# A two-part network on one core: an opening that starts its products early, meta tiles padded to 128 rows, and the last pair's norm taken head by head

## The reference, cut to what matters

```python
def first_block(...):                      # DEPTH = 2
    h = concatenate([meta, x], axis=1)     # 16 + 512 tokens
    for i in range(DEPTH):
        hn = rmsnorm(h, norm_w[i])
        h = h + (pool_mixer(hn, ...) if i == 0 else hgrn2_mixer(hn, ...))
    return rmsnorm(h[:, N_META:], final_norm_w)

def rmsnorm(x, w):
    return x * rsqrt(mean(x * x, -1) + EPS) * w

def pool_mixer(h, w_in, w_grp, scale, w_out):
    v, gate = split(h @ w_in, 2)           # 2 x 2048 columns, in 4 groups
    ...                                    # trailing means of v over 2, 4, 8 or 16 tokens, minus v
    return (u * silu(gate)) @ w_out

def hgrn2_mixer(h, w_in, lb, o_norm, w_out):
    q, fp, i_in, gate = split(h @ w_in, 4)  # 16 heads of 128
    # per head: gated linear attention in chunks, o = (scores @ v) + q * decay @ S
    o = o * rsqrt(mean(o * o, -1) + EPS)    # over each head's 128 values
    return (o * o_norm * silu(gate)) @ w_out
```

## Time and profile before

| | |
|---|---|
| median of 3 runs | 1637.94 us (1637.83 to 1638.79) |
| the profiled execution, its own time | 1639.15 us |
| its span, first to last instruction | 1637.3 us |
| TensorE busy | 1604.7 us (98%) |
| weight loads, VectorE, ScalarE, POOL busy | 85%, 60%, 34%, 24% |
| mean granted TensorE clock | 0.997 |

### The profile page before, as it was taken

One profiled execution on the slowest core, in us unless ns is written; L12 is line 12 of the kernel. 1 busy time (PEld: TensorE's weight loads), 2 busy tenths in 40 slices (PEclk: granted clock), 3 DMA queues, 4 the chain that ended last, 5 costly groups with the idle time before them and its releaser, 6 DMA issues.

```text
span 1637.3 us, 31100 instructions
## 1 busy us (share of the span) xinstructions
PE 1604.7 (98%) x12926; PEld 1398.9 (85%) x12926; DVE 989.8 (60%) x1524; ACT 548.9 (34%) x965; POOL 389.0 (24%) x344
## 2 busy tenths in 40 slices
PE   6999999999999999999999899999999999999998
PEld 5999999998888888889888688777888887778886
DVE  6757575765766568475675454557624845575446
ACT  4322222243243232324334333554112226451121
POOL 0000000020422124031431314327350043254510
PEclk9999999999999999999999999999999999999999
DMA  4323232323211312221222133222233242123331
GB/s 135 104 78 104 78 103 78 104 78 109 71 61 53 106 53 79 78 79 54 77 79 91 53 102 92 78 76 78 90 117 129 76 137 78 52 78 103 103 118 63
DMA packets 112619, 142.17 MB, mean 87 GB/s; under 512 B 3068, under 2 KB 88480, under 8 KB 112480
## 3 DMA queue, kind: packets, MB, share of 16 engines
q1 hardware_dynamic: 108368, 133.07, 25.4%
q10 hardware_dynamic: 4032, 6.89, 1.3%
q0 software_dynamic: 80, 0.20, 0.0%
HBM read 137.01 MB, written 2.10 MB: 85 GB/s over the span
## 4 chain that ended last, share of the span: by engine, by line
PE 93%; DVE 3%; ACT 2%; issue 1%; DMA 0%; SPq 0%; POOL 0%; DVEq 0%; ACTq 0%; POOLq 0%
PE acc L371 27%; PE acc L373 25%; PE acc L372 25%; PE aux L525 2%; PE aux L1098 1%; PE aux L1122 1%; PE aux L1109 1%; PE aux L371 1%; PE aux L372 1%; PE aux L373 1%; PE aux L552 1%; PE aux L550 1%; PE aux L511 1%; PE aux L542 1%; PE aux L430 0%
## 5 line engine op out<-in xcount | busy, mean ns | idle before, releaser
L371 PE MATMUL acc<-xhis,whi 128*128 128x264 f32 (+2 forms) x1888 | 627.9, 333 | 3.7 <-issue 1.1
L372 PE MATMUL acc<-xlos,whi 128*128 128x264 f32 (+2 forms) x1888 | 613.5, 325 | 0.0
L373 PE MATMUL acc<-xhis,wlo 128*128 128x264 f32 (+2 forms) x1888 | 613.5, 325 | 0.0
L371 PEld LDWEIGHTS acc<-xhis,whi 128*128 128x128 f32 x1888 | 355.4, 188 | 39.7 <-issue 7.1
L373 PEld LDWEIGHTS acc<-xhis,wlo 128*128 128x128 f32 x1888 | 355.5, 188 | 30.1
L372 PEld LDWEIGHTS acc<-xlos,whi 128*128 128x128 f32 x1888 | 355.8, 188 | 26.3
L366 POOL TENSOR_TENSOR wlo<-raw,whi 128x1024 fp32r<-128x1024 f32 x84 | 207.6, 2473 | 373.4 <-DVE whi L1931 373.4
L362 ACT ACTIVATE whi<-raw 128x1024 fp32r<-128x1024 f32 x160 | 165.9, 1048 | 152.8 <-PE acc L373 138.0
L366 DVE TENSOR_TENSOR wlo<-raw,whi 128x1024 fp32r<-128x1024 f32 x83 | 101.9, 1234 | 35.4 <-ACT whi L362 35.4
L1931 DVE CAST whi<-raw 128x1024 fp32r<-128x1024 f32 x84 | 66.3, 793 | 69.6 <-PE acc L373 66.6
L1728 DVE TENSOR_TENSOR wlo<-raw,whi 128x1024 fp32r<-128x1024 f32 x77 | 95.3, 1241 | 19.0 <-ACT whi L362 18.8
(11 more groups left out here) (281 smaller groups left out, 2644.0 us busy)
## 6 DMA issues: line engine op xcount, KB each, us to landing
raw<-in_w_in SPq DMA_DIRECT2D x38, 1024.0 KB, 5.1
raw<-in_hgrn_w_in SPq DMA_DIRECT2D x32, 1024.0 KB, 5.7
raw<-in_pool_w_in SPq DMA_DIRECT2D x16, 1024.0 KB, 5.4
raw<-in_pool_w_out SPq DMA_DIRECT2D x8, 1024.0 KB, 5.0
raw<-in_hgrn_w_out SPq DMA_DIRECT2D x8, 1024.0 KB, 5.1
raw<-in_w_out SPq DMA_DIRECT2D x8, 1024.0 KB, 5.0
raw<-in_pool_w_grp SPq DMA_DIRECT2D x4, 1024.0 KB, 5.2
raw<-in_w_branch_attn SPq DMA_DIRECT2D x4, 1024.0 KB, 4.9
```

Source lines behind the costliest of these rows:

```text
L371: pe.matmul(dst, stat[0], mov[0], start=first, stop=False)
L372: pe.matmul(dst, stat[0], mov[1], start=False, stop=False)
L373: return pe.matmul(dst, stat[1], mov[0], start=False, stop=last)
```

## The change

**Meta tiles of 128 rows.** `vtm` and `ktm` have 128 partitions in place of 16. POOL clears them once; ScalarE goes on writing their first 16 rows, and the matmul of L540 takes all 128.

**Last pair.** The norm is made head by head: squares, mean, reciprocal and root of head 0, its scaling by VectorE, then head 1 with scaling by ScalarE. A root of a dummy value is put behind the states' step. The second two pieces of weights are split by VectorE after level 7 instead of after level 6. In all pairs POOL's last level multiplies k of both heads before it combines their gates.

**b_out and the mean.** The last split and last gate product of the even pair (`held`) move behind the first addition to `h`. `mean_squares` runs within the second half of the first unit of stage B and not after it.

**Opening.** The identity and the norm weights are loaded first, then the first chunk of weights; the second waits for the last part of x. x comes in four parts of 256 features. TensorE begins with 14 matmuls on the matrix of ones. The sums of squares are taken by ScalarE along the rows of x (`row_squares`), 5 numbers per partition; the root and reciprocal are made of those, and a diagonal matrix times the matrix of ones (`spread_inverse`) gives `rstd`. The first two v units are made together, k-tile by k-tile as x comes in (`v_pair`). The gates' lower bounds are computed in stage A's first "out" part.

```diff
-            vtm = [sb(f"vtm{x}", [META, P], where=in_b) for x in range(2)]
+            vtm = [sb(f"vtm{x}", [P, P], where=in_b) for x in range(2)]
...
-            ktm = [sb(f"ktm{x}", [META, P], where=in_b) for x in range(2)]
+            ktm = [sb(f"ktm{x}", [P, P], where=in_b) for x in range(2)]
...
+                    if late is not None and n == 1 and k == K // 2 - 1:
+                        late()
...
-                    if first:
-                        mean_squares()
...
+            load_chunk(sp, 0, 0, w_in_a[:, :, 0:256], "k8", 0)
...
+                        if g == 0 and n == 1:
+                            sp.wait_ge(x_landed[3], 16)
...
+            for n in range(WARM):
+                pe.matmul(aux[:, n % 2, 0:P], ones_d[:, :], ones_d[:, :], start=True, stop=True)
...
+            def v_pair():
+
+                for k in range(6):
+                    turn(k)
+                pe.wait_ge(vec_ready, 1)
+                pe.wait_ge(meta_ready, 1)
+                pe.wait_ge(lo_ready, PA + 1 + CREDIT)
+                v_products(0, (0, 1))
+                turn(6)
+                v_products(0, (2, 3))
+                turn(7)
+                pe.wait_ge(lo_ready, PA + 2 + CREDIT)
+                v_products(1, (0, 1, 2, 3))
+                for tiles in ((4, 5), (6,)):
+                    for n in range(2):
+                        v_products(n, tiles)
+                spread_inverse()
+                for n in range(2):
+                    v_products(n, (7,)).then_inc(lin_done, 1)
+                vectors()
...
+            row_squares(0)
...
+            x_high(0)
+            x_high(1)
+            x_high(2)
+            split_hi(act, "k8", 0, 16, None)
+            x_high(3)
+            row_squares(1)
...
+                if s == LEVELS + 3:
+                    act.activation(spare[:, 1:2], ones_d[:, 0:1], ACT.Sqrt)
...
+                    if n == 0:
+                        held()
...
-                b_pair(i, "even", (2 * i + 1, 1), "k4")
-                b_out(UB + 24 + B_STEPS * i, PB + 24 + B_PIECES * i, True)
+                held = b_pair(i, "even", (2 * i + 1, 1), "k4", True)
+                b_out(UB + 24 + B_STEPS * i, PB + 24 + B_PIECES * i, True, held)
...
-                if s in (6, 7):
+                if s in (6, 8):
                     for m in range(2):
-                        split_lo_at(PO3, m + 2 * (s - 6), "vg")
+                        split_lo_at(PO3, m + s - 6, "vg")
```

More of the change, by code:

```diff
@@ L410, in weighted_lo, with root, inverse_vector, x_turned @@
                                      in1=xhi[:, k, :], op0=ALU.mult, op1=ALU.subtract).then_inc(xlo_ready, 1)
[L412 to L431, removed]
[L432 to L438 removed]
+        def root(act):
+            act.wait_ge(ms_ready, 2)
+            act.activation(rstd[:, :], rstd[:, :], ACT.Sqrt).then_inc(rstd_ready, 1)
+        def inverse_vector(dve):
+            dve.wait_ge(sq_used, 1)
+            dve.tensor_scalar(halves(rstd[:, :]), aux[:, :, 0:TH], EPS, None, ALU.add).then_inc(ms_ready, 1)
+            dve.wait_ge(ms_ready, 1)
+            dve.reciprocal(rstd[:, :], rstd[:, :]).then_inc(ms_ready, 1)
+            dve.wait_ge(rstd_ready, 1)
+        def x_turned(k):
+            return (aux, aux2)[k % 4 // 2][:, k % 2, :]
         def x_wait(pe, v):
@@ L555, in b_tensor_step @@
                 else:
-                    pe.wait_ge(on_ready, 1 + 2 * pair + x + 1)
+                    if z == "last" and x:
+                        pe.wait_ge(on_second, 1)
+                    else:
+                        pe.wait_ge(on_ready, 1 + 2 * pair + x + 1)
                     for c in range(CH):
@@ L878, in _ @@
                     pair = 2 * i + par
-                    for level in range(1, LEVELS + 1):
+                    for level in range(1, LEVELS):
                         for x in range(2):
@@ new lines, in spread_inverse, with v_products @@
+            def spread_inverse():
+                pe.wait_ge(h_ready, KT)
+                pe.wait_ge(diag_ready, 2)
+                pe.matmul(aux[:, 0, :], ones_d[:, :], diag[:, :, :].rearrange("p c t -> p (c t)"),
+                          start=True, stop=True)
+                pe.matmul(aux[:, 1, 0:META], ones_d[0:META, :], diag_m[:, :], start=True, stop=True)\
+                  .then_inc(spread, 1)
+            def v_products(n, tiles):
+                hi, lo = piece(whi, "k8", n), piece(wlo, "k8", n)
+                for k in tiles:
+                    pe.wait_ge(xlo_ready, k + 1)
+                    for half in range(2):
+                        mm = products(pe, acc[n][:, half, 0:TH], (hi[:, k, 0:P], lo[:, k, 0:P]),
+                                      of_x(k, TH * half, TH), k == 0, k == KT - 1)
+                return mm
@@ L1297, in _ @@
                         a_split(i, m)
+                    if stage == "out" and G == 0 and n == 4:
+                        act.wait_ge(lb_step, 3)
+                        act.activation(lbt[:, 3:5, :], lbt[:, 1:3, :], ACT.Exp).then_inc(lb_exp, 1)
                     if stage == "out" and G == NG - 1:
```

275 lines of the change are left out of this document (190 added, 85 removed).

## The result

| | before | after |
|---|---|---|
| median (times in the same set of runs) | 1638.15 us (1637.83 to 1638.79) | 1615.05 us (1614.13 to 1616.31) |
| ratio | | 0.9859, 95% interval 0.9842 to 0.9876 |
| the profiled execution, and its span | 1639.15, 1637.3 | 1616.31, 1614.5 |

The change makes the kernel 23.1 us faster by the medians and 22.8 by the spans. 1613.7 was predicted, with a range from 1609.5 to 1619.0.

What follows compares the result with a forecast made beforehand. TensorE, busy for 98% of the span, was taken as the bound. Terms of 6.2, 2.2, 1.0, 3.6, 3.4 and 7.8 sum to 24.2 us: 1639.15 becomes 1614.9, by the runs' median 1613.7; range 1609.5 to 1619.0.

Steps and rivals of the forecast that it cites:

- Meta tiles: At the four states of each head: 128 rows in place of 16 save 0.39 us per head, 16 times, 6.2 us.
- The pace of step 11: Two fp32 matmuls of 128 rows in 0.22 us, so a head's eight would take 0.89 us in place of 1.28.
- The rival from the Trainium skill's sentence: At the meta matmuls: 32 rows take as long as 128, so padding gives nothing, time 1619.9 us; chance 6%.
- b_out: At the third half unit of both `b_out`: TensorE's waits for the first addition to `h` go, 2.2 us; bounds 0 and 2.6.
- The mean: At stage B's third unit: the 0.99 us wait for `snb` goes, 1.0 us; bounds 0 and 1.2.
- Last pair, level 7: TensorE's k turns: VectorE's copy to `ab` ends earlier with the splits behind it, 3.6 us, some 1.7 of it half clock.
- The bound of 1.0 for "POOL's k as late as now": Lower bound of the level 7 gain, 1.0 us, if POOL's k for the second head comes no earlier.
- Last pair, norm: Norm's turns: table loaded before, head by head, 1.8 us, and full clock behind, 1.6 us; 3.4 in all, bounds 1.5 and 4.0.
- Opening: Stage A's start: VectorE sets the v part's pace, unit 7 starts at 57.3 against 65.1, 7.8 us; bounds 4.3 and 10.0.
- t: When VectorE takes the first v unit (first `vpad`): put at 31.0 us, bounds 28.8 and 34.5.
- The half clock at the products: In the opening: the first products begin at half clock after turns and gaps and lose 1.7 us.
- the rival with t = 34.5: The opening's products are late, VectorE takes the first v unit at 34.5 us, time 1617.2 us; chance 13%.

Runs made afterwards that it cites:

- the kernel with the early split: The kernel after without its 14 matmuls on ones, with the fourth weight piece split while VectorE and ScalarE wait for `rstd` to be spread; median 1613.50 us, ratio 0.9843.

## Why the prediction was right, point by point

- **Meta tiles**, 6.2 predicted, 6.2 measured. The pace of step 11, taken for matmuls whose rows don't change, was the right row. The rival from the Trainium skill's sentence falls.
- **b_out**, 2.2 predicted, 2.7 measured: the waits and the restart behind each. **The mean**, 1.0 predicted, 1.3 measured, the same way. Both are a tenth above the upper bounds that I gave.
- **Last pair, level 7**, 3.6 predicted, 3.7 measured. The size was right, and so was its half clock; the reason given was half of it. That the copy to `ab` came last let me treat POOL's new order as an aside, and it is a condition: alone, the late splits gain nothing. The bound of 1.0 for "POOL's k as late as now" should have been 0.
- **Last pair, norm**, 3.4 predicted, 3.5 measured. The turn of head 1 waits 1.14 us (1.5 forecast) and full clock holds. I had the preload as a full table load; it is worth 0.8 us.
- **Opening**, 7.8 predicted for unit 7, 6.7 measured: this term was sized too large, by 1.1 us. Its last two steps hold, 25.55 + 0.75 from `vpad` to unit 7 (25.55 + 0.75 measured), and the waits before units 5 to 7 are 0.5 us; the 1.08 us before unit 3 is above the 0.8 that I gave as the most. What failed is t, 32.16 for 31.0. The first product came at 15.79 for 14.5, because x's parts landed at 8.2, 11.0, 13.3 and 14.8 us, where the sum over bytes had half of x at 9.3 and all of it at 12. It was wrong in two ways. The loads begin more slowly than the 354 GB/s that it took from 2.5 us on: they move 174 and 222 GB/s from 2 to 4 us and some 300 until 7. And x's parts don't come one after another: by 11 us the windows add up to 2.8 MB, and not to the 2 MB of the weights and half of x, since the later parts were on their way too. (At 354 GB/s 2 MB would even be there by 8.4 us, so the 9.3 had some slack in it.) The chain behind the second part wasn't too short: 15.79 - 11.06 = 4.7 us, where 14.5 - 9.3 = 5.2 were summed, and from the first product to t it is 16.4 us where 16.5 were. The half clock at the products was foreseen with 1.7 us, and in this execution it was there, which is luck as far as the two executions at full pace go. Over the seven executions with this opening and 14 or no matmuls on ones, t lies between 30.3 and 32.2, so 31.0 is inside what this code does, and the rival with t = 34.5 isn't.
- **What was left out**: a drift of 0.5 to 0.6 us from unit 7 until 358 us in small steps, which all nine traces with the new opening show and whose cause stays open; and gaps of issuing.

The errors have both signs: +1.0 us on the small terms, -1.1 on the opening, -0.6 by drift, -0.5 by the gap. What is left of them, 1.2 us, is about the distance from 1613.7 to 1615.05. That it is so small is in part luck: terms missed by 1.1 and 0.5 us cancel.

## What to carry to other kernels

Set like instructions of two traces side by side and read where the lead changes: for one pair of executions it gave every place to 0.1 us, where medians of the parts were off by up to two. But unchanged code moved by up to 1.5 us in it too, so trust it at the places that the change touches. An engine that is named for a wait may be the victim of a third: look at what else stretched over the same stretch before you choose what to move, and move both. A narrow matmul between full ones costs its neighbours, so pad its rows where they are zero anyway.

## What the hardware showed that I had not expected

- **POOL and VectorE stop each other.** POOL's 256-column product took 3.06 us in place of 0.77 under two splits of VectorE, and VectorE's 528-column addition took 2.17 in place of 0.71 under one split of POOL. The Trainium skill (GPSIMD Engine Reference, 8. Key points) says that POOL shares its SBUF interfaces with VectorE and that they get in each other's way where VectorE has two inputs from SBUF. These rows agree and give the price: from 0.4 us (1.19 for 0.77, in the kernel before) up to nearly all of the other's instruction.
- **Half clock has no fixed price.** Behind the same wait of 2.9 us it lasted some 3 us in one execution, over 6 in a second and over 9 in a third, and at the first products it is there or not in the same code. By the traces this moves an execution by 1.5 us in the opening and by up to 3.3 in the last pair; in the ten executions of one kernel it shows as two groups, 3.7 us apart by their medians (mean clock 0.994 against 0.997). What decides it stays open.
- **The clock column can say 1.00 at half pace.** In the kernel with the early split 7 matmuls of 264 columns run per us from 17 to 18 us with 1.00 beside them; full pace is 11. In that trace the record of the clock begins only at 19.5 us, so the 1.00 before it isn't a reading. Read the pace too near the start.
- **Rows of 4 KB get more of the DMA than rows of 1 KB**, by two single executions. Beside the same weights all of x landed at 11.53 us by 4 KB and at 14.19 by 1 KB, with the weights 1.4 us later in return.
